# Hybrid state-space, attention and convolution layer on one core: a product in column tiles, and waits at three stage changes

## What is computed

```python
def hybrid_layer(x, ...):
    h = rms_norm(x, norm_pre)
    proj = h @ w_in                                  # 1024 x 11280
    (z, xbc, dt_raw, q, k, v, g_attn, u, b_sc, c_sc, g_sc, merge) = split(proj)
    y_ssm = ssd_branch(z, xbc, dt_raw, ...)          # conv, silu, chunked scan, gated norm
    y_attn = attention_branch(q, k, v) * silu(g_attn)   # 8 heads, 3 dilated windows (1, 4, 16)
    y_sc = b_sc * causal_conv(c_sc * u) * silu(g_sc)
    gates = sigmoid(merge).reshape(b, s, 3, 1024)
    merged = gates[0] * (y_ssm @ p_ssm) + gates[1] * (y_attn @ p_attn) + gates[2] * (y_sc @ p_sc)
    return x + rms_norm(merged @ w_out, norm_post)

def ssd_scan(xdt, a, b_in, c_in):                    # one step per chunk of 128 tokens
    y_diag = einsum("blgn,bsgn->blsg", cc, bc) * decay matrix, times xc
    y_off = einsum("blgn,bgjpn,blgj->blgjp", cc, state, exp(cs))
    state = state * exp(cs[-1]) + einsum(bc, exp(cs[-1] - cs), xc)
```

## Time and profile before

| what | value |
|---|---|
| median of 3 runs | 2852.78 us |
| lowest and highest run | 2850.05 and 2854.59 us |
| the profiled execution, its own time | 2852.36 us |
| its span, first to last instruction | 2850.7 us |
| PE busy | 2760.1 us, 97% of the span |
| DVE, ACT, POOL busy | 1581.4, 1238.0, 1576.6 us (55%, 43%, 55%) |
| mean granted clock of PE | 0.987 of full speed |
| projection, scan, attention, merge and output, by the first PE instruction of each | from 0, 1524.9, 1976.3, 2281.4 us |

### The profile page before, as it was taken

One profiled execution on the slowest core, in us unless ns is written; L12 is line 12 of the kernel. 1 busy time (PEld: TensorE's weight loads), 2 busy tenths in 40 slices (PEclk: granted clock), 3 DMA queues, 4 the chain that ended last, 5 costly groups with the idle time before them and its releaser, 6 DMA issues. The chain is left out here.

```text
span 2850.7 us, 44158 instructions
## 1 busy us (share of the span) xinstructions
PE 2760.1 (97%) x15998; PEld 2295.0 (81%) x15998; DVE 1581.4 (55%) x2527; ACT 1238.0 (43%) x2258; POOL 1576.6 (55%) x1078
## 2 busy tenths in 40 slices
PE   6999999999999999999998999999999889999998
PEld 5888888888887888888887788887988777778787
DVE  6335334897544346885424555555777686743433
ACT  5232234333224533332234565565777654532332
POOL 7677778877777788777773454553111254322000
PEclk8999999999999999999999999999999999999999
DMA  3556345433225345332135454555665478855543
GB/s 125 142 171 216 132 133 154 129 117 96 69 72 192 118 150 148 112 110 74 60 119 185 150 187 149 191 171 168 188 204 177 126 247 257 297 186 171 170 148 110
DMA packets 462813, 436.24 MB, mean 153 GB/s; under 512 B 60736, under 2 KB 403008, under 8 KB 454976
## 3 DMA queue, kind: packets, MB, share of 16 engines
q1 hardware_dynamic: 460352, 425.79, 47.7%
q0 software_dynamic: 2304, 8.39, 0.8%
HBM read 290.99 MB, written 143.13 MB: 152 GB/s over the span
## 5 line engine op out<-in xcount | busy, mean ns | idle before, releaser
L550 PE MATMUL p_acc<-h_kept,w_hi 128*128 128x512 f32 x1216 | 475.4, 391 | 4.6 <-ACT work L596 3.1
L552 PE MATMUL p_acc<-h_kept,w_lo 128*128 128x512 f32 x1216 | 474.1, 390 | 0.0
L551 PE MATMUL p_acc<-h_kept,w_hi 128*128 128x512 f32 x1216 | 474.1, 390 | 0.0
L431 POOL TENSOR_TENSOR w_lo<-p_sums,w_hi 128x512 fp32r<-128x512 f32 x300 | 390.8, 1319 | 131.4 <-ACT w_hi L637 131.4
L637 ACT ACTIVATE w_hi<-p_sums 128x512 fp32r<-128x512 f32 x300 | 189.0, 632 | 471.8 <-PE p_acc L552 449.0
L550 PEld LDWEIGHTS p_acc<-h_kept,w_hi 128*128 128x128 f32 x1216 | 228.8, 188 | 53.9 <-ACT work L596 3.3
L552 PEld LDWEIGHTS p_acc<-h_kept,w_lo 128*128 128x128 f32 x1216 | 228.8, 188 | 47.6
L551 PEld LDWEIGHTS p_acc<-h_kept,w_hi 128*128 128x128 f32 x1216 | 228.9, 188 | 47.1
L550 PE MATMUL p_acc<-p_ops,w_hi 128*128 128x512 f32 x608 | 238.0, 391 | 7.1 <-DVE p_ops L738 7.1
L551 PE MATMUL p_acc<-p_ops,w_hi 128*128 128x512 f32 x608 | 237.3, 390 | 0.0
L552 PE MATMUL p_acc<-p_ops,w_lo 128*128 128x512 f32 x608 | 237.1, 390 | 0.0
(11 more groups left out here) (344 smaller groups left out, 6725.2 us busy)
## 6 DMA issues: line engine op xcount, KB each, us to landing
raw<-w_in SPq DMA_DIRECT2D x100, 512.0 KB, 4.7
s_qs<-p_stage SPq DMA_DIRECT2D x96, 256.0 KB, 3.9
work<-s_gates SPq DMA_DIRECT2D x48, 512.0 KB, 7.3
p_rawb<-w_in SPq DMA_DIRECT2D x38, 512.0 KB, 3.7
keep<-w_in SPq DMA_DIRECT2D x38, 512.0 KB, 4.8
s_xbc<-p_stage SPq DMA_DIRECT2D x32, 512.0 KB, 2.6
work<-s_xbc SPq DMA_DIRECT2D x16, 1024.0 KB, 6.4
spare<-s_qs SPq DMA_DIRECT2D x16, 1024.0 KB, 5.7
```

What stands on the lines that cost most here:

```text
L431: tt(w_lo[:, k], weight(u, k), w_hi[:, k], ALU.subtract).then_inc(w_made, 1)
L550: pe.matmul(bank, hi, ops[k][:, 0, c], start=c == 0, stop=False)
L551: pe.matmul(bank, hi, ops[k][:, 1, c], start=False, stop=False)
L552: last = pe.matmul(bank, lo, ops[k][:, 0, c], start=False, stop=c == 3)
```

## The change

There are three parts. **One**: the product `c_t * state` is made by `matmul_by_columns`. **Two**, at the changes of stage: the last set's two stores signal a semaphore of their own, `last_stored`, for which SP waits only ahead of the scan's last pair of chunks; the unit for the scan is split into slot 0 rather than 2, after the set's second product, ahead of the copy of B12 (and the scan's slots are renumbered); the wait for the gate stores is moved to POOL in the attention stage, behind the four pieces of `split_first_lo`; and `load_ahead` is called ahead of the store of pattern g = 1 rather than g = 2. **Three**: `evacuate_v` waits for g = 1 until `o_made` is 48 * pair - 4 rather than 48 * pair + 1.

```diff
+GATES_STORED = 3 * DM // P + 1
 def projection_stage(...):
-                            sp.dma_start(d[kind][2 * i + m, :, tokens], stage[:, slot]).then_inc(stored[slot], 16)
+                            sp.dma_start(d[kind][2 * i + m, :, tokens], stage[:, slot]
+                                         ).then_inc(stored[slot] if u < NSETS - 1 else last_stored, 16)
...
-                    sp.wait_ge(stored[slot], 16 * stores_before(NSETS, slot))
+                    sp.wait_ge(stored[slot], 16 * stores_before(NSETS - 1, slot))
...
-                flat_hi, flat_lo = (x[:].rearrange("p k n -> p (k n)")[:, 2 * DM:3 * DM] for x in (w_hi, w_lo))
+                flat_hi, flat_lo = (x[:].rearrange("p k n -> p (k n)")[:, :DM] for x in (w_hi, w_lo))
...
-                act.wait_ge(b12_loaded, 16)
-                act.activation(op_flat(1, 0), op_flat(1, 1).bitcast(F32), ACT.Copy).then_inc(b12_hi, 1)
                 act.wait_ge(unit_loaded, 32)
-                act.wait_ge(prod, PRODUCTS * NSETS - 1)
-                act.activation(w_hi[:].rearrange("p k n -> p (k n)")[:, 2 * DM:3 * DM], raw[1].rearrange("p c n -> p (c n)"),
+                act.wait_ge(prod, PRODUCTS * (NSETS - 1) + 2)
+                act.activation(w_hi[:].rearrange("p k n -> p (k n)")[:, :DM], raw[1].rearrange("p c n -> p (c n)"),
                                ACT.Copy).then_inc(unit_hi, 1)
+                act.wait_ge(b12_loaded, 16)
+                act.activation(op_flat(1, 0), op_flat(1, 1).bitcast(F32), ACT.Copy).then_inc(b12_hi, 1)
 def ssd_gates_stage(...):
+                sp.wait_ge(first["kv_stored"], 32)
                 chunks(PAIRS - 1, True)
-                for j in range(2):
-                    sp.wait_ge(g_stored[j], 16 * UNITS + 16)
...
-                            slot = (j // 2 + 2) % 3
+                            slot = j // 2 % 3
...
-                            pe.matmul(ps_y[:, g % 2, 1], c_t[:, g], state[:, g * GW:(g + 1) * GW], start=True,
-                                      stop=True).then_inc(y_made, 1)
+                            matmul_by_columns(pe, ps_y[:, g % 2, 1], c_t[:, g], state[:, g * GW:(g + 1) * GW], start=True,
+                                              stop=True).then_inc(y_made, 1)
 def attention_stage(...):
-                eng.wait_ge(o_made, NS * (pair - (g == 0)) + {0: 4 * SPAN + 4, 1: 1, 2: 4}[g])
+                eng.wait_ge(o_made, NS * (pair - (g == 0)) + {0: 4 * SPAN + 4, 1: -4, 2: 4}[g])
...
                             load_q(i + 1, 0, 2 * i + 2, g)
-                        elif g == 2:
+                        elif g == 1:
                             load_ahead()
                         store(i, g)
...
                     split_first_lo(pool, n)
+                for j in range(2):
+                    pool.wait_ge(first["g_stored"][j], 16 * GATES_STORED)
                 for i in range(PAIRS):
```

More of the change, by code:

```diff
@@ L166, in padded, with projection_stage @@
     return kind in ("q", "xbc", "sc")
-def projection_stage(nc, w, d, kept, wt, v, v_all, ident, eps, spare, keep):
+def projection_stage(nc, w, d, kept, wt, v, v_all, ident, eps, spare, keep, last_stored):
     BPREP, TSTEP, DT, CHAIN = 1, 9, (41, 44), 46
@@ L1026, in ssd_gates_stage @@
         stored, carried = first["y_out"], s.sem("s_carried")
-        raw_loaded, w_hi_made, g_stored = s.sem("s_raw_loaded"), s.sem("s_whi_r"), s.sems("s_g_stored", 2)
+        raw_loaded, w_hi_made, g_stored = s.sem("s_raw_loaded"), s.sem("s_whi_r"), first["g_stored"]
         y_made = s.sem("s_y_made")
@@ L1136, in chunks @@
                         if k == 0:
-                            split(3 * i + 2, 1)
+                            split(3 * i + 2, 2)
                         elif not last:
-                            split(3 * i + 3, 2)
-                            split(3 * i + 4, 0)
+                            split(3 * i + 3, 0)
+                            split(3 * i + 4, 1)
                 pool.sem_inc(xd_made, 1)
@@ L1237, in _ @@
                 act.sem_inc(loaded[0], 16)
-                act.activation(w_hi[:, 0], raw[:, 0], ACT.Copy).then_inc(w_hi_made, 1)
+                act.activation(w_hi[:, 1], raw[:, 0], ACT.Copy).then_inc(w_hi_made, 1)
                 for j in range(2):
@@ L1309, in _ @@
                 dve.wait_ge(w_hi_made, 1)
[L1310 removed]
+                dve.tensor_tensor(w_lo[:, 1], raw[:, 0], w_hi[:, 1].bitcast(F32), ALU.subtract).then_inc(w_made, 1)
                 dve.wait_ge(norm_loaded, 16)
@@ L2486, in build @@
         first = {n: s.sem("first_" + n + "_loaded") for n in ("v", "k", "q0", "q1")}
-        first["y_out"] = s.sem("scan_y_stored")
+        first["y_out"], first["g_stored"], first["kv_stored"] = (
+            s.sem("scan_y_stored"), s.sems("scan_g_stored", 2), s.sem("last_kv_stored"))
         with ExitStack() as inner:
@@ L2496, in build @@
             v.update({"tri": k.sb("v_tri", [P, P]), "ones": k.sb("v_ones", [P, P]), "dskip": dskip})
-            projection_stage(nc, w, d, kept, wt, v, v_all, ident, eps, spare, keep[:])
+            projection_stage(nc, w, d, kept, wt, v, v_all, ident, eps, spare, keep[:], first["kv_stored"])
             ssd_gates_stage(nc, w, d, kept, wt, v, ident, eps, spare, keep[:], first)
```

5 lines of the change are left out of this document (2 added, 3 removed).

## The result

| | before | after |
|---|---|---|
| median of the runs, us | 2852.78 (2850.05 to 2854.59) | 2833.32 (2824.56 to 2837.06) |
| ratio, 95% interval | | 0.9923 (0.9907 to 0.9939) |
| profiled execution, its span, us | 2852.36, 2850.7 | 2827.95, 2826.3 |

The change takes 19.5 us off the median; the forecast was 2830.5, and the range from 2823 to 2841 holds it. The profiled execution is among the quicker of its kernel, so its trace has to explain 24.4 us.

The account below looks back on a forecast made before the run. PE, busy for 97% of the span, was taken as the bound. Gains of 10.7 + 2.3 + 2.4 + 6.9 + 0 = 22.3 us from 2852.36 gave 2830.1, stated as 2830.5 for the median; asked range 2823 to 2841.

Parts of the forecast that it names:

- two pairs, each 0.216: 0.43 in all: Scan: the state product split by columns streams as two pairs of passes, 0.43 us in all.
- 0.35 for two groups: Scan: PE saves 0.35 us per two groups, mostly by not switching to the whole array and back; 32 times.
- 10.7: Scan: total gain in us forecast for the state product in column tiles, with ends of 8 and 13.4.
- the overhead of each added instruction: Scan's state products: some 60 cycles per added matmul, estimated at 3.2 us, making the sum 7.5 rather than 10.7.
- after the second group nothing is gained: Scan: behind the second group the switch to the gates' whole array only moves behind the state product; 0.92 us as before.
- Only one chunk shows a real stop. I leave it as it is: Scan: only the second chunk has PE waiting, 3.49 us for DVE's normalised y; taken as unchanged.
- Each chain keeps its distance to PE: Scan: each chain from the last group to the turned result keeps its distance to PE; PE's chunk 0.7 us shorter.
- POOL and DVE slow each other; with a shorter chunk they meet more often: Scan rival: another engine sets the chunk's pace; state product brings 2 rather than 10.7 us, 2839.2; chance 0.12.
- The 11 us of slack in each chunk: Scan: argument against the rival that another engine sets the pace; chunk 27 us, DVE busy 14.9, ACT 15.9, POOL 15.5.
- 2.3, 2.4 and 4.86: Barriers from projection to scan, scan to attention, attention to merge: us earlier; the last grows to 6.9 at the first turn.
- The announced stops of 3.6, 3.0 and 2.3 us: Sign of being right: PE's stops at the three stage changes, which were 5.87, 5.39 and 7.19 us.
- Zero was said: Attention's copies of values: DVE's 4.5 us of waiting counted as no gain, since PE did not stand still; ends 0 and 2.

Follow-up runs that it names:

- e10: e9 with the state product as one whole matmul again; 2829.0 us, ratio 0.9926 to the kernel before.
- e9: Changed kernel with three waits on POOL, so both weight splits of a chunk run in gaps between DVE's two-SBUF-operand operations; 2822.6 us, ratio 0.9900.
- e1: Kernel before with only the scan's state product in column tiles; 2856.2 us, ratio 0.9987.
- e2: Changed kernel with the state product as one whole matmul again; 2849.8 us, ratio 0.9963.
- e4: Changed kernel run once more as it is, on another chip; 2843.6 us, ratio 0.9948.
- e7: Changed kernel where POOL also waits for ACT's root before the second weight split of the odd chunks; 2841.4 us, ratio 0.9932.
- e8: Changed kernel, POOL's second split waiting for DVE's normalised result, with the merge-stage loads back behind the second pattern's store; 2838.7 us, ratio 0.9921.
- e12: Kernel before with e9's three waits on POOL's splits and nothing of the change; 2843.1 us, ratio 0.9968.
- e5: Changed kernel, POOL's second split waiting for DVE's normalised result, with the next weight unit's load issued ahead of the sums; 2831.5 us, ratio 0.9900.
- e6: Changed kernel, POOL's second split waiting for DVE's normalised result, with the state's update in column tiles too; 2833.7 us, ratio 0.9905.
- e11: Changed kernel with the second weight unit's load issued ahead of the two gate stores in odd chunks; 2832.5 us, ratio 0.9936.

## Why the prediction was right, and where it was not

**The state product.** The step "two pairs, each 0.216: 0.43 in all" holds (0.43), and "0.35 for two groups" came out as 2.95 - 2.61 = 0.34. Its sum, "10.7", was mis-sized: a chunk got 0.56 us shorter and not 2 x 0.34 = 0.68, so the term measured 8.7. I had compared the groups with what stands beside them and not one whole chunk with the next. The gate matmuls behind each pair of groups follow each other more slowly: from the second to the twelfth their starts lie 2.29 us apart in e10 and 2.33 in e9, and the rest is spread over other runs of gate matmuls. Why, no run here shows. This is not the overhead of each added instruction by which the prediction works out 7.5 beside its 10.7: that would have left 0.25 us for two groups, and they gained 0.34. That "after the second group nothing is gained" holds: from the last small pair to the second gate matmul it is 0.93 us in both kernels.

**Who waits in the scan.** The step that failed is "Only one chunk shows a real stop. I leave it as it is": one execution was read as if its stops were the kernel's. Six executions in which nothing held the splits back (the kernel before, the changed one, e1, e2, e4, e7) lost 7.3 to 19.3 us to them in fourteen chunks, with the state product in either form. The scan's 7.9 us in the two profiles are 8.7 by the chunks' length, less 2.4 lost to one stop more, and 1.7 gained at the start of the scan. There PE waited 1.96 us for ACT's copy of x in the kernel before and 0.51 in the changed one; in the other kernels this wait ranges from none to 2.27, so that gain is luck. "Each chain keeps its distance to PE" was right for DVE's: its sum of y and the skip begins at +8.1 us of a chunk and not at +8.9, the turned result is due at +17.0 and not at +17.6. It was wrong for POOL's first split, which follows its load and stayed where it was, so that the sum now meets it in 14 chunks of 16 and not in 3. The rival that names the mechanism ("POOL and DVE slow each other; with a shorter chunk they meet more often") had its first half, for the sum of y and the skip, and the wrong price for it: the 8.7 us of the first part were not eaten down to 2. How many of the long stops the shorter chunk adds, two executions with the whole product (one and four of them) and four with the columns (two each) can't tell. The 11 us of slack in each chunk were no argument in either direction: a stop needs one late operation and not a busy engine, and in the earlier trace rows DVE's busy time contains what it stands in front of POOL.

**The stage changes.** 2.3, 2.4 and 4.86 were forecast; PE's stops are shorter by 2.22, 2.50 and 4.94, and the first turn's further 2.04 came as 2.11. The announced stops of 3.6, 3.0 and 2.3 us are 3.65, 2.89 and 2.25. The merge's first turn is 20.6 us earlier and not 22: the scan fell 2.8 short, and 1.2 of the projection came by chance. e8 shows that the last of them hangs on where the loads are issued.

**Part three.** Zero was said, and nothing else is seen: DVE's idle time of 4.5 us before these copies is gone, and attention lasts 298.2 us after 297.9. e1 and e12, which do not have this part, have the 4.5 us and an attention of 298.0 and 297.2. With the part it ranges from 295.2 to 301.5, so up to 2 us, the end that the prediction gave, can't be ruled out. The row of these copies now, to set beside the earlier trace rows:

```profile
L1495 DVE COPY a_vt<-a_pst 128x512 f32<-128x512 f32 x45 | 30.8, 687 | 0.3 <-POOL a_bandruns L1602 0.2
```

**The total.** Against the profile, 22.3 stood for 24.4: 10.7 became 7.9, part two gave 11.7 for 11.6, and 5.0 at both ends of the program came by chance. The timed median is 19.5 below before: if 11.7 of that are part two's, 7.8 are left for the first part and for the difference in stops. That the median came within 3 us of the 2830.5 is in part luck, since the stops alone make 12 us between one execution and another. What kept the forecast near is part two, where every term was a distance between two rows.

## What to carry to other kernels

A group whose longest instance is five times its median, with a mean that looks harmless, is worth a look before the costliest groups are: find what ran beside the long ones, and ask how often a second execution would show it. When a chain is moved earlier, ask which of its neighbours moves with it and which stays, since it hangs on something else (here POOL's split, on a load). If two engines exclude each other, place the one with slack by a wait in the other's gap: here three waits on POOL, which had ample time, brought as much as a rewritten product on the engine that sets the pace. And column tiles on a full-size product pay where they save a switch between the array's forms, and cost one where they add it.

## What the runs showed of the hardware

- A DVE operation with two SBUF operands waits for a whole POOL operation that is under way: 0.69 us became 2.75 (e5), 0.48 became 2.56 and 1.23 became 3.17 (the changed kernel). Those with an operand in PSUM kept their 1.22 beside POOL (e9). POOL waits likewise when DVE is first: 2.40 became 3.37 (e4).
- Two halves of the array by columns stream side by side at 256 columns of float32 too: 0.43 us for two pairs of passes. A switch there and back costs 0.32 to 0.35 us among gate matmuls (e6 against e9).
- A stop of PE of 3.44 us was followed by 3.4 us at 1.2 GHz and cost 5.3 us in all, and the one of 3.49 us in the kernel before by 6.8 us at 1.2 GHz and cost 6.4. Its length does not tell whether that follows: it did behind stops of 2.27 us (e11, second chunk) and 2.74 (e2, fourth), and not behind 2.82 (the changed kernel, tenth) and 3.37 (e2, fourteenth), which cost 3.0 and 3.6.
